# Two weight-remainder subtractions of the even mixer's output projection, moved from VectorE to GpSimd

## The chip, the cores and the metric

The kernel runs on one core of a Trainium2 chip. The metric is the device time of one execution in microseconds (us), the median of several runs. The core has five engines that work side by side and wait for one another through semaphores: TensorE (PE) for matmuls, VectorE (DVE), ScalarE (ACT), GpSimd (POOL) and SyncE (SP), which here only issues DMAs. SBUF is the working memory that all of them share; PSUM takes the matmul results, and its eight banks are called `ps` here.

## The reference

Two layers over 256 latent tokens and 256 context tokens of width 1024. Each layer is a half-step SwiGLU FFN, a mixer and a second half-step FFN. The even layer's mixer is the stage of this study:

```python
pl = hl @ w_in
a_l = silu(layernorm(depthwise_conv31(val * sigmoid(gate)) + b))   # 512 channels
q, k = rope(...); att_l = softmax(q k^T, window, context, sink) v  # 8 heads of 64
yl = concatenate([a_l, att_l]) @ w_out
```

The same is done for the context tokens. Everything is float32.

## The kernel before

**Products in three parts.** A float32 product is made of three faster ones. Both factors are split in a rounded high part (type fp32r) and the remainder: `hn_hi`, `hn_lo` for activations, `w_hi`, `w_lo` for weights. `three` (L491 to L493) issues hi by hi, lo by hi, hi by lo.

**Units of weights.** Weights come in units of up to 128 x 2048 elements. SP loads unit u into `raw[:, u % 2]` (L399), and waits for `lo_made >= u - 1` first, since the slot must be free. ACT copies it to `w_hi[:, u % 2]` (`head`, L989, semaphore `hi_made`), and DVE subtracts, `w_lo = raw - w_hi` (`rest`, `rest_of`, L1304, semaphore `lo_made`). PE waits for `lo_made` before it uses a unit. `E` is the first of the seven units of the even mixer's input projection, `E + 7` to `E + 10` are the four units of its output projection (`U["ev_out"]` is `E + 7`). They are used only after the attention and the LayerNorm of the convolution.

**The convolution.** 512 channels are four tiles of 128. Each of the 31 taps of tiles 0, 1 and 2 is one DVE instruction on 128 x 512 (`taps`, L1509 for a tile's first tap, L1512 for the others): `y = upad * weight + y`. The taps are issued in a fixed order, some ahead of the attention loop and some two or three at a time within it. Tile 3 is done by PE (`conv_turn`, L743): for each tap a matmul of a 128 x 128 diagonal of weights. GpSimd makes the 31 diagonals (`tensor_scalar` on the identity, L480) into 12 places. Diagonal n from 12 on waits until PE has used diagonal n - 12 (`turned_tap`).

**Before the attention.** DVE works through a list written out by hand: batches of taps, the rotary embedding, `w_lo` of units E + 4, E + 5, E + 6, then 12 taps, `gated_value(2)` (L1498, the gated input of tile 2), `w_lo` of E + 7, 12 taps, `gated_value(3)`, `w_lo` of E + 8, the negated sinks (L1553), and then the attention loop.

**The attention loop.** 16 steps j, one for a head pair, a stream and a query tile. In step j PE computes the scores of j + 1 (L706), two taps of tile 3 (L743) from j = 1 on, the transposes of step j - 1's weights (L720) and, in some steps, the products with the values (L734). DVE takes the row maxima (`largest`: L1563 or L1568, then L1570, which releases ACT), the denominators (L1577, L1578) and some taps. ACT computes the exponentials (L1130), normalises (L1143) and copies the transposes (L1152).

Of the kernel before, what the change touches and what calls it, by code (L numbers as in the profile page):

```python
# [44 lines left out]
ALU = mybir.AluOpType  # L45
# [17 lines left out]
def schedule():  # L63

    base, size = {}, []

    def add(name, n, elements):
        base[name] = len(size)
        size.extend([elements] * n)

    def ffn(name):
        for part, n in zip("AB", PARTS):
            add(f"{name}up{part}", n, UNIT)
            add(f"{name}down{part}", KT, n * P)

    ffn("f0")
    add("ev_in", 7, UNIT)
    add("ev_out", 4, UNIT)
    ffn("f1")
    ffn("f2")  # L80
    add("od_gate", 1, KT * 4 * HM)
    add("od_in", 16, UNIT)
    add("od_out", 4, UNIT)
    ffn("f3")
    return base, size


def build(nc, t, out):

    U, SIZE = schedule()  # L90
    NU = len(SIZE)
    with ExitStack() as ctx:
        def sb(name, shape, dt=F32, scope=ctx):
            return scope.enter_context(nc.sbuf_tensor(name, shape, dt))

        def sem(name):
            return ctx.enter_context(nc.semaphore(name))
# [5 lines left out]
        raw = sb("raw", [P, 2, UNIT])  # L103
        w_hi = sb("w_hi", [P, 2, UNIT], F32R)
        w_lo = sb("w_lo", [P, 2, UNIT], F32R)
# [55 lines left out]
        hi_made = sem("hi_made")  # L161
        lo_made = sem("lo_made")
# [122 lines left out]
        def bank(u, j=0):  # L285
            return 2 * (u % 2) + j
# [4 lines left out]
        def col(name, i, n=1):  # L291
            return cols[:, COLS[name][0] + i:COLS[name][0] + i + n]
# [35 lines left out]
        DIAGS = 12  # L328

        def diag_place(n):  # L330
            q = n % DIAGS
            return (acc, sd, rstd)[q // 4][:, q % 4 * P:(q % 4 + 1) * P]
# [126 lines left out]
        @block.gpsimd  # L459
        def _(pool):  # L460
            def vector_rows(i):

                q = i % SLOTS_MOD
                pool.dma_start(mod_raw[:, q, :], t["mod_w"][i]).then_inc(mod_in[q], 16)  # L464

            for i in range(SLOTS_MOD):
                pool.wait_ge(mod_mm, 5 + i // 2)
                vector_rows(i)
            pool.wait_ge(mod_mm, KT)
            pool.dma_start(c_row.rearrange("p s k -> p (s k)"), t["c_rows"].partition_broadcast(P))\  # L470
                .then_inc(c_rows_in, 16)
            for i in range(SLOTS_MOD, MOD_F0 + SLOTS_MOD):
                pool.wait_ge(mod_made, KT + i - SLOTS_MOD + 1)
                vector_rows(i)
            pool.wait_ge(mats_in, 16)
            pool.wait_ge(rstd_mm, 2)
            for n in range(CONV_W):
                if n >= DIAGS:
                    pool.wait_ge(turned_tap, n - DIAGS + 1)
                pool.tensor_scalar(diag_place(n), ident, col("conv_w", n * CT + 3), None, ALU.mult).then_inc(diag_ready, 1)  # L480
            for i in range(MOD_F0 + SLOTS_MOD, NMOD):
                pool.wait_ge(mod_made, KT + i - SLOTS_MOD + 1)
                vector_rows(i)
# [808 lines left out]
        def _(dve):  # L1292
# [8 lines left out]
            def rest(u0, r, n):  # L1301

                dve.wait_ge(hi_made, u0 + 2 * r + 1)
                dve.tensor_tensor(w_lo[:, u0 % 2, 0:n], raw[:, u0 % 2, 0:n], w_hi[:, u0 % 2, 0:n],  # L1304
                                  ALU.subtract).then_inc(lo_made, 1)

            def rest_of(u):
                if u < NU:
                    rest(u, 0, SIZE[u])
# [178 lines left out]
            E = U["ev_in"]  # L1488
# [5 lines left out]
            def gated_value(c, gate, b):  # L1494

                u = E + c if c < 2 else E + 3 + c
                dve.wait_ge(gate_made, CONV_G + c + 1)
                dve.tensor_tensor(upad[:, c, :, PAD:PAD + LAT], two_streams(gate), two_streams(ps[:, b, :]),  # L1498
                                  ALU.mult).then_inc(unit_evac, 1)

            def taps(a, b):

                for n in range(a, b):
                    c, i = TAP_ORDER[n]
                    if i == 0 and c in (0, 2):
                        dve.wait_ge(unit_evac, E + 2 if c == 0 else E + 6)
                    dst, src = two_streams(y[:, c, :]), upad[:, c, :, i:i + LAT]
                    if i == 0:
                        ins = dve.tensor_scalar(dst, src, col("conv_w", c), col("conv_b", c), ALU.mult, ALU.add)  # L1509
                    else:  # L1510
                        dve.wait_ge(tap_done, TAP_AT[c, i - 1] + 1)
                        ins = dve.scalar_tensor_tensor(out=dst, in0=src, scalar=col("conv_w", i * CT + c), in1=dst,  # L1512
                                                       op0=ALU.mult, op1=ALU.add)
                    ins.then_inc(tap_done, 1)
# [30 lines left out]
            rest_of(E + 6)  # L1545
            taps(EARLY, EARLY + 12)
            gated_value(2, t_ring[:, 0, :], bank(E + 5))
            rest_of(E + 7)
            taps(EARLY + 12, AHEAD_OF_LOOP)
            gated_value(3, t_ring[:, 1, :], bank(E + 6))  # L1550
            rest_of(E + 8)

            link(dve.tensor_scalar(att_cols[:, 4, 0:NH_ATT], col("sink", 0, NH_ATT), -1.0, None, ALU.mult))  # L1553

# [76 lines left out]
            u = U["od_gate"]  # L1631
# [4 lines left out]
            for d, s, tiles_of in ((0, 0, rows[:, 0, :, 2:4]), (0, 2, rows[:, 0, :, 0:2]), (1, 0, rows[:, 1, :, ::-1])):  # L1636
                n = tiles_of.shape[2]
# [106 lines left out]
            for n in range(16):  # L1744
                u = U["od_in"] + n
# [196 lines left out]
```

## Time and profile before

| | |
|---|---|
| median of 3 runs | 1844.24 us (1844.22 to 1845.74) |
| the profiled execution | 1850.17 us, of which the span is 1848.4 us |
| busy share of the span | PE 97%, DVE 62%, ACT 33%, POOL 5% |
| TensorE's granted clock, mean | 0.982 |
| the stage of the change, from the first gated value to the last attention product | 432 to 581 us of the span |

The span runs from the first to the last instruction of the profiled execution. Busy shares are means over stages with different limits, so a small edit has to be read from the stage in which it lies. Starts are in us from the beginning of the span. An instruction that follows another on its engine overlaps it a little in the records, so one of a row is read off the starts as well as the durations.

### The profile page before, as it was taken

Reading aid. Unit: us, or ns where it says so; the run is one execution under the profiler, and the core shown is the slowest. Engines: PE = TensorE matmul, PEld = TensorE weight load, DVE = VectorE, ACT = ScalarE, POOL = GpSimd, SP = SyncE. Lnnn points to the kernel's source line nnn. Section 1 sums busy time; section 2 is a strip of 40 time slices with the busy share of each in tenths; the row PEclk is TensorE's granted clock in tenths of the full one; section 3 lists DMA queues with packets and bytes.
Section 4 is the critical chain, followed back from the end, with each engine's and each line's share of the span. In section 5 each row is a group of like instructions: output and inputs, shape, how many; then the busy total and the mean of one; then the engine's idle time right before and its main releaser. Section 6 shows DMA issues by size and latency. Waiting matters only on the chain.

```text
span 1848.4 us, 23459 instructions
## 1 busy us (share of the span) xinstructions
PE 1787.1 (97%) x9265; PEld 1489.0 (81%) x9265; DVE 1142.1 (62%) x1735; ACT 617.0 (33%) x821; POOL 96.9 (5%) x164
## 2 busy tenths in 40 slices
PE   9999999999899999999999999999999999899996
PEld 5888888878545778888888788888888999899996
DVE  5578667875964557766787577433346436765554
ACT  4332223232375333212322322122223333454342
POOL 0011001020030001000110010000000000000000
PEclk8999999999899999999999999999999999999998
DMA  9455455542200225555555254332222222245552
GB/s 386 157 193 181 170 183 185 187 168 78 82 1 1 74 90 196 174 183 175 193 171 178 88 187 141 108 109 96 72 90 85 76 69 92 91 147 178 178 177 95
DMA packets 49040, 253.36 MB, mean 137 GB/s; under 512 B 5568, under 2 KB 7104, under 8 KB 32576
## 3 DMA queue, kind: packets, MB, share of 16 engines
q1 hardware_dynamic: 30384, 184.10, 28.8%
q0 software_dynamic: 18576, 68.17, 11.5%
q8 instruction: 54, 0.88, 0.2%
q14 instruction: 26, 0.21, 0.0%
HBM read 251.20 MB, written 1.05 MB: 136 GB/s over the span
## 4 chain that ended last, share of the span: by engine, by line
PE 88%; DVE 6%; ACT 4%; issue 1%; DMA 1%; SPq 0%; ACTq 0%; DVEq 0%
PE ps L491 27%; PE ps L493 27%; PE ps L492 27%; DVE w_lo L1304 2%; ACT w_hi L989 1%; DVE y L1512 1%; PE ps L857 1%; PE ps L886 1%; PE ps L743 1%; PE ps L720 1%; PE ps L521 1%; PE ps L734 1%; DVE t_ring L1360 0%; PE ps L706 0%; PE ps L546 0%
## 5 line engine op out<-in xcount | busy, mean ns | idle before, releaser
L491 PE MATMUL ps<-hn_hi,w_hi 128*128 128x512 f32 (+2 forms) x1784 | 645.0, 362 | 14.5 <-DVE hn_lo L1367 7.2
L492 PE MATMUL ps<-hn_lo,w_hi 128*128 128x512 f32 (+2 forms) x1784 | 638.7, 358 | 0.0
L493 PE MATMUL ps<-hn_hi,w_lo 128*128 128x512 f32 (+2 forms) x1784 | 638.5, 358 | 0.0
L1304 DVE TENSOR_TENSOR w_lo<-raw,w_hi 128x2048 fp32r<-128x2048 f32 (+2 forms) x184 | 376.9, 2048 | 349.2 <-ACT w_hi L989 349.0
L989 ACT ACTIVATE w_hi<-raw 128x2048 fp32r<-128x2048 f32 (+2 forms) x184 | 316.5, 1720 | 732.8 <-PE ps L493 726.5
L491 PEld LDWEIGHTS ps<-hn_hi,w_hi 128*128 128x128 f32 (+1 forms) x1784 | 337.9, 189 | 72.7 <-DVE hn_lo L1367 10.0
L493 PEld LDWEIGHTS ps<-hn_hi,w_lo 128*128 128x128 f32 (+1 forms) x1784 | 337.8, 189 | 50.1
L492 PEld LDWEIGHTS ps<-hn_lo,w_hi 128*128 128x128 f32 (+1 forms) x1784 | 337.8, 189 | 48.2 <-issue 0.5
L491 PE MATMUL ps<-a_hi,w_hi 128*128 128x512 f32 (+1 forms) x704 | 255.6, 363 | 2.6 <-DVE a_lo L1434 1.7
L492 PE MATMUL ps<-a_lo,w_hi 128*128 128x512 f32 (+1 forms) x704 | 255.3, 363 | 0.0
L493 PE MATMUL ps<-a_hi,w_lo 128*128 128x512 f32 (+1 forms) x704 | 255.2, 363 | 0.0
L1408 DVE CUSTOM_DVE_ANT_0 t_ring<-mod_raw,cols 128x1024 f32<-128x1024 f32 x128 | 163.9, 1280 | 1.8
L1408 DVE CUSTOM_DVE_ANT_0 mod_raw<-mod_raw,cols 128x1024 f32<-128x1024 f32 x128 | 163.9, 1281 | 0.0
L491 PEld LDWEIGHTS ps<-a_hi,w_hi 128*128 128x128 f32 x704 | 132.9, 189 | 23.6 <-DVE a_lo L1434 2.1
L493 PEld LDWEIGHTS ps<-a_hi,w_lo 128*128 128x128 f32 x704 | 132.9, 189 | 20.7
L492 PEld LDWEIGHTS ps<-a_lo,w_hi 128*128 128x128 f32 x704 | 132.9, 189 | 20.6
L1323 DVE SCALAR_TENSOR_TENSOR xT<-ps,modT,xT 128x256 f32<-128x256 f32 x136 | 59.9, 479 | 133.0 <-PE ps L493 132.9
L1048 ACT ACTIVATE a_hi<-prod 128x512 f32 (+3 forms) x88 | 50.9, 579 | 212.8 <-DVE prod L1431 212.8
L464 POOL DMA_DIRECT2D mod_raw<-in_mod_w x128 | 67.8, 530 | 900.8 <-DVE modT L1408 859.5
L1434 DVE TENSOR_TENSOR a_lo<-prod,a_hi 128x512 fp32r<-128x512 f32 (+1 forms) x88 | 55.0, 625 | 63.6 <-ACT a_hi L1048 63.6
L491 PE MATMUL ps<-w_hi,hn_hi 128*128 128x256 f32 x256 | 76.0, 297 | 0.0
L493 PE MATMUL ps<-w_hi,hn_lo 128*128 128x256 f32 x256 | 72.4, 283 | 0.0
(214 smaller groups left out, 1305.2 us busy)
## 6 DMA issues: line engine op xcount, KB each, us to landing
raw<-in_w_up SPq DMA_DIRECT2D x88, 1024.0 KB, 4.9
mod_raw<-in_mod_w POOLq DMA_DIRECT2D x128, 512.0 KB, 3.8
raw<-in_w_downA SPq DMA_DIRECT2D x32, 768.0 KB, 4.2
raw<-in_w_downB SPq DMA_DIRECT2D x32, 640.0 KB, 3.9
raw<-in_w_od_in SPq DMA_DIRECT2D x16, 1024.0 KB, 4.9
mod_raw<-in_mod_first SPq DMA_DIRECT2D x8, 1024.0 KB, 9.5
raw<-in_w_ev_in SPq DMA_DIRECT2D x7, 1024.0 KB, 5.1
raw<-in_w_ev_out SPq DMA_DIRECT2D x4, 1024.0 KB, 5.0
```

The source lines that it names most:

```text
L464: pool.dma_start(mod_raw[:, q, :], t["mod_w"][i]).then_inc(mod_in[q], 16)
L491: pe.matmul(o, lh, rh, start=first, stop=False)
L492: pe.matmul(o, lh, rl, start=False, stop=False)
L493: return pe.matmul(o, ll, rh, start=False, stop=last)
L521: last = pe.matmul(ps[32 * g:32 * g + 32, BLOCK_BANKS[b % 2], 0:LAT], c_act[:, 2 * g + i, :], block_place(b)[:, 2 * g + i, :], start=(i == ...
L720: last = pe.transpose(ps[:, 6 + h2, i * P:(i + 1) * P], weight_place(s)[:, h2, i * P:(i + 1) * P], ident)
L989: act.activation(w_hi[:, u0 % 2, 0:n], raw[:, u0 % 2, 0:n], ACT.Copy).then_inc(hi_made, 1)
L1048: act.activation(a_hi[:, j + 2 * r, 0:w], prod[:, j, 0:w], ACT.Copy).then_inc(a_hi_made, 1)
L1304: dve.tensor_tensor(w_lo[:, u0 % 2, 0:n], raw[:, u0 % 2, 0:n], w_hi[:, u0 % 2, 0:n], ALU.subtract).then_inc(lo_made, 1)
L1323: last = dve.scalar_tensor_tensor(out=xT[:, d0 + 2 * r, tokens(s)], in0=ps[:, bank(u0, b), tokens(s)], scalar=modT[:, vec, d0 + 2 * r, s:s ...
L1408: last = dve.tensor_tensor_reduce(out=spent, in0=mod_raw[:, q, :], in1=c_row[:, s, :], scale=1.0, scalar=col("mod_b", m * KT + k), op0=ALU ...
L1434: dve.tensor_tensor(a_lo[:, j + 2 * r, 0:w], prod[:, j, 0:w], a_hi[:, j + 2 * r, 0:w], ALU.subtract).then_inc(a_made, 1)
```

## The change

The subtractions for units E + 7 and E + 8 leave DVE's list. GpSimd makes them, one ahead of diagonal 12 and one ahead of diagonal 13. Each waits for the `lo_made` of the unit before and for ACT's `w_hi` of its own unit.

```diff
@@ gpsimd
             for n in range(CONV_W):
+                if n in (DIAGS, DIAGS + 1):
+                    u = U["ev_out"] + n - DIAGS
+                    pool.wait_ge(lo_made, u)
+                    pool.wait_ge(hi_made, u + 1)
+                    pool.tensor_tensor(w_lo[:, u % 2, :], raw[:, u % 2, :], w_hi[:, u % 2, :],
+                                       ALU.subtract).then_inc(lo_made, 1)
                 if n >= DIAGS:
                     pool.wait_ge(turned_tap, n - DIAGS + 1)
@@ vector
             taps(EARLY, EARLY + 12)
             gated_value(2, t_ring[:, 0, :], bank(E + 5))
-            rest_of(E + 7)
             taps(EARLY + 12, AHEAD_OF_LOOP)
             gated_value(3, t_ring[:, 1, :], bank(E + 6))
-            rest_of(E + 8)
```

## Rows read from the trace of the kernel before

**Rows 1.** The page: the chain that ended last, by engine

```profile
PE 88%; DVE 6%; ACT 4%; issue 1%; DMA 1%; SPq 0%; ACTq 0%; DVEq 0%
```

**Rows 2.** The chain in order of time, 487 to 507 us (start, us, what)

```profile
487.40 2.20 DVE w_lo L1304
...
497.94 2.20 DVE w_lo L1304
...
503.90 3.71 PE ps L743 x4
```

**Rows 3.** Busy us and count by engine in stretches, then granted clock, DMA share, GB/s

```profile
488.00:490.00 2.00, 2.00 (x10) 1.65 (x10) 2.00 (x3) 0.00 (x0) 0.00 (x0) 1.00 0.00 0
...
498.00:500.00 2.00, 0.00 (x0) 0.00 (x0) 2.00 (x1) 0.00 (x0) 0.00 (x0) 0.50 0.00 0
...
506.00:508.00 2.00, 2.00 (x5) 0.83 (x5) 1.93 (x9) 0.53 (x1) 0.90 (x2) 0.50 0.00 0
508.00:510.00 2.00, 1.94 (x11) 1.15 (x9) 1.16 (x2) 1.10 (x3) 0.85 (x1) 0.96 0.00 0
```

**Rows 4.** Timeline of ACT ahead of the loop (start, us, instruction)

```profile
480.01 1.91 ACT L989 ACTIVATE w_hi<-raw 128x2048 fp32r<-128x2048 f32 x1
491.64 0.60 ACT L1119 ACTIVATE t_ring<-ps 128x512 f32<-128x512 f32 x1 [9.72 <-PE ps L493]
...
494.05 1.28 ACT L1130 ACT_TABLE_LOAD   x1
```

**Rows 5.** Timeline of DVE ahead of the loop

```profile
478.77 8.03 DVE L1512 SCALAR_TENSOR_TENSOR y<-upad,cols,y 128x512 f32<-128x512 f32 x12
486.72 0.68 DVE L1498 TENSOR_TENSOR upad<-t_ring,ps 128x512 f32<-128x512 f32 x1
```

**Rows 6.** Timelines of POOL and DVE where a diagonal meets DVE's work

```profile
403.64 2.12 POOL L480 TENSOR_SCALAR acc<-mats,cols 128x128 f32<-128x128 f32 x1 [13.35 <-PE ps L558]
```

```profile
403.00 2.29 DVE L1304 TENSOR_TENSOR w_lo<-raw,w_hi 128x2048 fp32r<-128x2048 f32 x1 [0.83 <-ACT w_hi L989]
```

**Rows 7.** The same where DVE's instruction is the longer one, with its undisturbed like

```profile
536.22 0.60 POOL L480 TENSOR_SCALAR acc<-mats,cols 128x128 f32<-128x128 f32 x1 [0.26 <-PE ps L743]
```

```profile
536.27 0.86 DVE L1512 SCALAR_TENSOR_TENSOR y<-upad,cols,y 128x512 f32<-128x512 f32 x1
```

```profile
537.06 0.74 DVE L1512 SCALAR_TENSOR_TENSOR y<-upad,cols,y 128x512 f32<-128x512 f32 x1
```

```profile
517.38 0.78 DVE L1512 SCALAR_TENSOR_TENSOR y<-upad,cols,y 128x512 f32<-128x512 f32 x1
```

```profile
407.47 0.66 DVE L1367 SCALAR_TENSOR_TENSOR hn_lo<-t_ring,modT,hn_hi 128x256 fp32r<-128x256 f32 x1
```

```profile
409.35 0.48 DVE L1367 SCALAR_TENSOR_TENSOR hn_lo<-t_ring,modT,hn_hi 128x256 fp32r<-128x256 f32 x1
```

**Rows 8.** Timeline of all engines in the loop's first steps

```profile
506.00 0.60 POOL L480 TENSOR_SCALAR acc<-mats,cols 128x128 f32<-128x128 f32 x1 [92.38 <-PE ps L743]
...
507.39 0.16 DVE L1570 SCALAR_TENSOR_TENSOR att_cols<-att_cols 128x2 f32<-128x2 f32 x1
...
507.71 1.15 POOL L480 TENSOR_SCALAR acc<-mats,cols 128x128 f32<-128x128 f32 x1 [1.10 <-PE ps L743]
...
508.90 0.72 ACT L1130 ACTIVATE prod<-gact,att_cols 128x512 f32<-128x512 f32 x1 [2.37 <-PE ps L720]
```

**Rows 9.** Timeline of PE: taps at full clock, taps 12 and 13, first output unit

```profile
529.71 1.99 PE L743 MATMUL ps<-upad,rstd 128*128 128x512 f32 x4
...
534.14 1.13 PE L743 MATMUL ps<-upad,acc 128*128 128x512 f32 x2
```

```profile
584.10 0.80 PE L491 MATMUL ps<-hn_hi,w_hi 128*128 128x512 f32 x1
```

**Rows 10.** Timelines of SP and ACT: loads of E + 9, E + 10, first copy

```profile
489.63 10.87 SPq L399 DMA_DIRECT2D raw<-in_w_ev_out  x2
```

```profile
606.86 1.92 ACT L989 ACTIVATE w_hi<-raw 128x2048 fp32r<-128x2048 f32 x1 [2.61 <-PE ps L493]
```

## The prediction

> **What bounds the kernel now.** I read first the page's chain of work that ended last. It is 88% PE and 6% DVE [rows 1], so an edit on DVE is worth time only where DVE has its few per cent of the chain. The chain in order of time shows that this place is one of them. From 487 to 500 us it lies on DVE without a break, and both subtractions that the change removes are pieces of it, 2.20 us each [rows 2]. The table of stretches says the same from the other side: at 488 to 490 us PE is still full, at 498 to 500 us PE, ACT and POOL do nothing at all, DVE is full, and TensorE's granted clock has gone to 0.50 [rows 3]. So the start of the attention loop hangs on the DVE list alone.
>
> **Removed.** Two instructions by 2.20 us is 4.40 us. Is all of it there to be had? The next limits ahead of the loop are ACT's: the sigmoid for `gated_value(3)` starts at 491.64 us and lasts 0.60, and the load of the table for the exponential ends at 494.05 + 1.28 = 495.33 us [rows 4]. The loop can start when the second subtraction ends, at 497.94 + 2.20 = 500.14 us [rows 2]; 4.40 us earlier is 495.74, still behind both. So removal alone would give all 4.40 us, and the loop behind it is a chain of dependent steps that would start and end so much earlier.
>
> **Added, the first subtraction.** GpSimd has been idle since its twelfth diagonal. It starts when ACT's `w_hi` of E + 7 is there, at 480.01 + 1.91 = 481.92 us [rows 4]. DVE is then in a batch of 12 taps, 478.77 to 486.80 us [rows 5], each with two inputs in SBUF. Do the two engines disturb each other? The rows show two things. A diagonal that normally takes 0.60 us took 2.12 us when it started inside DVE's 2.29 us subtraction, and ended at 405.76, some 0.5 us after it [rows 6]. So GpSimd waits for a DVE instruction with two SBUF inputs. The other way round, the tap that begins as GpSimd reads takes 0.86 us against 0.74, another one 0.78 us, and an `hn_lo` piece 0.66 us against 0.48 [rows 7]. So a diagonal's read of 128 elements costs DVE 0.04, 0.12 or 0.18 us. The new instruction reads two inputs of 2048, 32 times as many elements: 1.3, 3.8 or 5.8 us. I take the middle, 3.8 us, and keep the other two for the range; below them stands no cost, if GpSimd fits its reads into the pauses between DVE's instructions. For the upper end there is also the whole 0.60 us of a diagonal by 16 for the length alone, 9.6 us. A block of B us here delays the taps and everything behind them by B, as DVE has no idle time up to the loop. With 3.8 us the start of the loop is at -4.4 + 3.8 = -0.6 us.
>
> The rows don't say whether DVE loses only the cycles of the reads or the whole of GpSimd's instruction. The Trainium skill, "SBUF — State Buffer", says that the pair of ports the two engines share is an exclusive lock for a whole instruction, also between a GpSimd instruction that reads SBUF and a DVE one with two SBUF inputs, and that whoever starts first keeps it. The skill's "GPSIMD Engine Reference" (section 3.1) gives 4497 ns for a two-input instruction of 2048 float32 elements, and advises VectorE for such work. No row of this trace has that instruction; by the page the block would be about 4.2 us as an estimate and the whole sum 0.8 us worse than mine.
>
> **Added, the second subtraction.** It stands behind diagonal 12, and that waits for PE's first tap, which is inside the loop. Diagonal 12 started at 506.00 us, with 0.26 us between two diagonals the next instruction would start at 506.86 us [rows 7, 8]. I let its reads begin 0.3 us later. DVE's instructions on PSUM and one SBUF input go on, but L1570 at 507.39 us [rows 8] has two SBUF inputs and waits: until 506.86 + 0.3 + 3.8 = 510.96, which is 3.57 us. Queued behind it on DVE are the denominators of step 1 and two taps; and ACT waits for L1570 with the exponentials of step 2, and PE with its transposes for ACT. These exponentials started at 508.90 us, held by PE's transposes and not by DVE [rows 8]; L1570 ended at 507.55, so 1.35 us of slack cover it. What is left is 3.57 - 1.35 = 2.2 us on the chain PE to ACT to PE, which has no later pause to make it up. In general the second block costs B - 1.6 us, and nothing below 1.6.
>
> **The diagonals behind.** Diagonal 13 came at 507.71 us and would come at about 511.5. PE uses the diagonals 12 and 13 at 534.14 us [rows 9], so some 20 us cover the delay; without this cover each us late would be a us of the loop. If GpSimd had to fetch code for another kind of instruction, that would be covered too.
>
> **The weights.** `w_lo` of E + 7 is first needed when PE begins the output projection at 584.10 us [rows 9], 70 us after the later of the two subtractions. SP's load of E + 9 waits for the first subtraction and that of E + 10 for the second: issues at 489.63 and 500.17 us now [rows 10], the latter would be at about 511. ACT copies E + 9 at 606.86 us [rows 10]. Nothing is queued behind these loads that is wanted earlier. Cost zero, covered by 90 us.
>
> **TensorE's clock.** It stood at 0.50 (1.2 GHz) in the stretches from 498 to 508 us, and was 0.96 in 508 to 510 [rows 3]. At that level the four matmul records of the first two taps cost 3.71 us on the chain [rows 2], and the same four at full clock 1.99 us [rows 9]. A stall in step 2 may keep the clock low for the next two taps too: up to 1.7 us. An earlier loop start might win a part of the low stretch. I put nothing in the sum and both in the range.
>
> **The sum.** -4.4 (removed) + 3.8 (first block) + 2.2 (second block past its slack) = +1.6 us. In general it is 2B - 6.0 us, zero at B = 3.0. The durations are from the profiled execution, 1850.17 us with a span of 1848.4 and 1.8 us around it; it lies 5.9 us above the median of the runs, which I take as a constant of the profiler. On the median: 1844.24 + 1.6 = 1845.8 us.
>
> **Rivals.**
> - *GpSimd slips into DVE's pauses.* GpSimd is the one that waits, and DVE keeps its pace; the diagonals inside tap batches lengthened few taps and by little [rows 7], which speaks for it. Against it: a diagonal reads 128 elements and may just fit a pause, 4096 can't. With no delay 1844.24 - 4.4 = 1839.8 us; with 0.12 us on each of the 12 taps 1841.3; with B = 1.3 us, 1841.1. It ends beyond 0.2% only with less than 0.7 us of delay in all.
> - *The block is long.* One mechanism: DVE stands still while GpSimd reads, at 482 and at 507 us. From B = 4.9 us on the sum is over +3.7 us. At 5.8 us it is -4.4 + 5.8 + 4.2 = +5.6, 1849.8 us; at 9.6 us +13.2, 1857.4 us. For it speaks the `hn_lo` row [rows 7], against it the two tap rows.
> - *The clock stays low in step 2.* On top of my forecast: 1845.8 + 1.7 = 1847.5 us.
> - *The change does nothing*, since the attention's start hangs on something else. Only PE, idle, and ACT, done at 495.33, are there [rows 3, 4]. 1844.2 us, hardly possible.
>
> **How the numbers follow.** A change of 0.2%, 3.7 us, is about what a measurement of this kernel can tell from none. Forecast (B between 1.6 and 4.9 us, with or without the clock's part): 0.5. GpSimd in the pauses: 0.25, of which 0.17 with nearly no delay. The long block: 0.22. No effect: 0.03. So faster 0.18, same 0.56, slower 0.26 (0.04 of it from the clock on top of the forecast). The range reaches down to the gain without any block, 1839.8, and up to the block of 5.8 us, 1849.8. The likeliest case alone spans 1841.5 to 1848.
>
> **What would show it.** In the profile after: the two GpSimd instructions at about 482 and 506 to 507 us; a gap or one long tap of about 3.8 us in DVE's batch of 12 (right), or 12 taps in 8.0 us as now (the first rival); the loop's first L1563 at about 499.6 us (495.8 for the first rival); L1570 of step 2 held to about 510.5, and the exponentials behind it waiting for DVE and not for PE. I am wrong if GpSimd's instruction takes much more than 5 us, if DVE runs through it, or if GpSimd gets its turn only when the tap batch is over.

## The result, and the profile after

The changed kernel takes 1848.57 us (median of 20 runs, 1843.9 to 1853.87) against 1844.37 us (20 runs, 1841.83 to 1849.25): a ratio of 1.0020, with a 95% interval of 1.0013 to 1.0027. That is 3.7 us slower (2.4 to 5.0) by the ratio, 4.2 us by the medians. The forecast was +1.6 us. The time lies in its range, but 1.2 us from the upper end of it (1849.8), and 0.6 us above the 1848 up to which I had put the likeliest case alone. The loss is also at the 3.7 us from which I had reckoned the long block.

Everything that the prediction spoke of stands in the timelines between 475 and 510 us. Lines 476 on are moved by the edit: L486 of after is L480 of before, L1310 is L1304, L1504 is L1498, L1515 and L1518 are L1509 and L1512, L1567 is L1563, L1574 is L1570, L1136 is L1130, L749 is L743; L482 is the new subtraction. Kernels with other edits are moved by a few lines more. First GpSimd (start, us, instruction, what ended the idle time before it):

```profile
480.48 9.22 POOL L482 TENSOR_TENSOR w_lo<-raw,w_hi 128x2048 fp32r<-128x2048 f32 x1 [68.43 <-ACT w_hi L995]
503.55 0.78 POOL L486 TENSOR_SCALAR acc<-mats,cols 128x128 f32<-128x128 f32 x1 [13.85 <-PE ps L749]
504.30 4.51 POOL L482 TENSOR_TENSOR w_lo<-raw,w_hi 128x2048 fp32r<-128x2048 f32 x1
508.79 2.59 POOL L486 TENSOR_SCALAR acc<-mats,cols 128x128 f32<-128x128 f32 x3
```

Then VectorE over the same stretch:

```profile
475.00 2.28 DVE L1310 TENSOR_TENSOR w_lo<-raw,w_hi 128x2048 fp32r<-128x2048 f32 x1
477.20 8.04 DVE L1518 SCALAR_TENSOR_TENSOR y<-upad,cols,y 128x512 f32<-128x512 f32 x12
485.14 0.69 DVE L1504 TENSOR_TENSOR upad<-t_ring,ps 128x512 f32<-128x512 f32 x1
485.87 4.12 DVE L1515 TENSOR_SCALAR y<-upad,cols 128x512 f32<-128x512 f32 x1
...
497.99 0.69 DVE L1567 CUSTOM_DVE_ANT_0 gact<-ps,att_mask 128x512 f32<-128x512 f32 x1
...
505.12 3.72 DVE L1574 SCALAR_TENSOR_TENSOR att_cols<-att_cols 128x2 f32<-128x2 f32 x1
```

And ScalarE's exponentials of step 2, which in [rows 8] waited for PE:

```profile
508.87 0.72 ACT L1136 ACTIVATE prod<-gact,att_cols 128x512 f32<-128x512 f32 x1 [4.61 <-DVE att_cols L1574]
```

The reader is to see three things. GpSimd alone needs 4.51 us for what VectorE does in 2.28; its first subtraction took 9.22 us, because it got nothing while the 12 taps ran, which kept their 8.04 us [rows 5]. It was served behind them, beside `gated_value(2)` (489.70 - 4.51 = 485.19 us, an estimate), and then VectorE's tensor_scalar lasted 4.12 us instead of 0.54. That tensor_scalar reads one 128 x 512 tensor and a column of weights, so an instruction needn't read two large tensors from SBUF to be held; `gated_value(2)`, with one input in SBUF and one in PSUM, took its usual 0.69 us. The second one stopped an instruction on two columns, L1574, for 3.72 us instead of 0.16, up to the end of GpSimd's instruction (504.30 + 4.51 = 508.81; 505.12 + 3.72 = 508.84).

The table of stretches of after has a piece that was not in before (stretch and its length in us; busy us and count of PE, its weight loads, VectorE, ScalarE, GpSimd; then TensorE's granted clock, DMA share, GB/s): PE idles while it waits for step 2, and the clock falls to 0.50 once more.

```profile
508.00:510.00 2.00, 0.70 (x2) 0.00 (x0) 1.97 (x5) 1.14 (x3) 2.00 (x3) 1.00 0.39 53
510.00:512.00 2.00, 0.00 (x0) 0.00 (x0) 1.93 (x6) 2.00 (x7) 1.38 (x2) 1.00 0.70 274
512.00:514.00 2.00, 1.40 (x6) 0.76 (x8) 1.45 (x3) 1.13 (x4) 0.00 (x0) 0.84 0.48 201
514.00:516.00 2.00, 2.00 (x5) 0.50 (x2) 0.89 (x3) 2.00 (x7) 0.00 (x0) 0.50 0.00 0
```

### The profile page after: what moved, and what is told of

Read it like the earlier page. It is cut to its first block, busy times and chain, and to the rows that moved or that the text cites. A ratio compares the mean times of both kernels' runs of the same rounds, so it can differ in the third digit from the quotient of the medians.

```text
span 1849.8 us, 23461 instructions
## 1 busy us (share of the span) xinstructions
PE 1784.0 (96%) x9265; PEld 1487.6 (80%) x9265; DVE 1145.1 (62%) x1733; ACT 617.1 (33%) x821; POOL 109.9 (6%) x166
## 4 chain that ended last, share of the span: by engine, by line
PE 87%; DVE 6%; ACT 4%; DMA 1%; issue 1%; SPq 0%; ACTq 0%; DVEq 0%
PE ps L497 27%; PE ps L498 27%; PE ps L499 27%; DVE w_lo L1310 1%; ACT w_hi L995 1%; DVE y L1518 1%; PE ps L863 1%; PE ps L892 1%; DMA mod_raw<-in_mod_first 1%; PE ps L749 1%; PE ps L726 1%; PE ps L740 1%; PE ps L552 1%; PE ps L712 0%; DVE t_ring L1366 0%
## 5 line engine op out<-in xcount | busy, mean ns | idle before, releaser
L1310 DVE TENSOR_TENSOR w_lo<-raw,w_hi 128x2048 fp32r<-128x2048 f32 (+3 forms) x182 | 372.4, 2046 | 347.7 <-ACT w_hi L995 347.5
```

## A ruler for the stage

Single profiles reach this stage up to 4.6 us apart, so I measure within it. The ruler has four parts, taken as differences of starts in each kernel's timelines: **a** from `w_lo` of E + 6 to the loop's first L1563; **b** from there to the exponentials of step 2; **c** from there to those of step 4; **d** from there to the LayerNorm's first VectorE instruction. **Stage** ends at the first residual of the output projection (L1323, 606.87 us in before) and contains 22.2 us more. For before, a is 500.26 - 476.57 = 23.69. Ratios are to the runs of the kernel before on the same chip.

| kernel | a | b | c | d | stage | ratio (95% interval) |
|---|---|---|---|---|---|---|
| before | 23.69 | 8.64 | 8.86 | 66.94 | 130.30 | |
| before_again | 23.70 | 7.52 | 8.86 | 66.93 | 129.25 | 0.9996 (0.9986 to 1.0005) |
| after | 22.99 | 10.88 | 9.96 | 66.94 | 132.97 | 1.0020 (1.0013 to 1.0027) |
| after_again | 23.77 | 10.88 | 9.96 | 66.94 | 133.75 | 1.0020 (1.0009 to 1.0031) |
| no_sub | 19.50 | 7.65 | 8.86 | 66.93 | 125.15 | 0.9980 (0.9971 to 0.9989) |
| first_only | 25.97 | 8.13 | 8.87 | 66.93 | 132.13 | 1.0021 (1.0011 to 1.0031) |
| second_only | 21.50 | 10.88 | 9.90 | 66.93 | 131.41 | 1.0021 (1.0013 to 1.0030) |
| dve_in_loop | 19.41 | 8.10 | 8.85 | 66.93 | 125.52 | 0.9979 (0.9970 to 0.9987) |
| half | 21.56 | 8.72 | 8.86 | 66.94 | 128.28 | 0.9995 (0.9987 to 1.0004) |
| pieces | 19.91 | 7.52 | 8.85 | 66.95 | 125.46 | 0.9977 (0.9967 to 0.9987) |
| after_busy | 23.77 | 10.89 | 8.87 | 66.93 | 132.67 | 1.0006 (0.9997 to 1.0014) |
| write_only | 19.42 | 7.71 | 8.86 | 66.94 | 125.13 | one run |
| one_input | 22.80 | 10.00 | 11.35 | 66.94 | 133.31 | one run |

Part d is the same in all: behind step 4 nothing of the change is left. What the change does lies in a, b and c. Outside of the stage the profiles differ too, without a pattern by edit: 471.9 to 476.6 us ahead of it and 1237 to 1244 us behind it.

## The experiments

**What there was to win (no_sub).** Edit of before:

```diff
+            def mark_of(u):
+                dve.wait_ge(hi_made, u + 1)
+                dve.tensor_tensor(w_lo[:, u % 2, 0:8], raw[:, u % 2, 0:8], w_hi[:, u % 2, 0:8],
+                                  ALU.subtract).then_inc(lo_made, 1)
...
-            rest_of(E + 7)
+            mark_of(E + 7)
...
-            rest_of(E + 8)
+            mark_of(E + 8)
```

> The two subtractions shrink to 8 of 2048 columns and stay on VectorE in their old places; the rest of the work of these two units is left out, GpSimd gets nothing. This shows how much there was to win. Theory 1 (the loop's start hangs on VectorE's list, both 2.20 us pieces are on the chain): 4.1 us faster than before, about 1840.3, the first L1563 4.1 us earlier after w_lo of E+6. Rival (something else holds the loop's start, so nothing was ever to be had, and the change only added waits): 0 to 1 us faster.

1840.3 us, 3.7 us faster (2.0 to 5.3). Part a fell by 4.19 us, as the two shortened pieces ask. So the loop's start does hang on VectorE's list and all of it comes through to the end; "the change does nothing" falls, and so does a gain that something else holds back.

**The first subtraction alone (first_only).** Edit of after:

```diff
-                if n in (DIAGS, DIAGS + 1):
+                if n == DIAGS:
...
             gated_value(3, t_ring[:, 1, :], bank(E + 6))
+            dve.wait_ge(lo_made, E + 8)
+            rest_of(E + 8)
```

> Only the subtraction ahead of diagonal 12 is GpSimd's, the one of E+8 stays on VectorE in its old place. Theory 1 (VectorE's tensor_scalar stands still for 3.6 us, 2.2 us won): 1.4 us slower than before, about 1845.8. Rival (the first block costs nothing, all of the loss is in the loop): 2.2 us faster.

Here GpSimd was served in the middle of the 12 taps. Timeline of VectorE, then of GpSimd:

```profile
475.93 12.38 DVE L1518 SCALAR_TENSOR_TENSOR y<-upad,cols,y 128x512 f32<-128x512 f32 x12
```

```profile
479.22 5.23 POOL L482 TENSOR_TENSOR w_lo<-raw,w_hi 128x2048 fp32r<-128x2048 f32 x1 [66.87 <-ACT w_hi L995]
```

The batch of taps lasts 12.38 us instead of 8.04: a hold of 4.3 us, against 2.2 us saved. Part a is 2.28 us longer, where 1.4 was expected from the first profile's 3.6. The hold is 4.3 us in both; in after 0.7 us of it lay beside `gated_value(2)` (485.14 to 485.83 us), which has one SBUF input and was not stopped. The rival, a first block for nothing, falls. By the ratio the kernel is 3.9 us slower (2.0 to 5.7); its stage is 1.8 and 2.9 us longer than in the two profiles of before.

**The second alone (second_only).** Edit of after:

```diff
-                if n in (DIAGS, DIAGS + 1):
+                if n == DIAGS + 1:
...
+            rest_of(E + 7)
             taps(EARLY + 12, AHEAD_OF_LOOP)
```

> Only the subtraction ahead of diagonal 13 is GpSimd's, the one of E+7 stays on VectorE in its old place. Theory 1 (L1570 of step 2 waits 3.6 us, 2.2 us of it past the slack, 2.2 us won ahead of the loop, and TensorE's clock falls once more after the stall for about 1 us): 0 to 1.3 us slower than before, 1844.4 to 1845.7. Rival (the whole loss of the change comes from the clock that falls in the stall): 2.5 us slower or more.

Part a is 2.20 us shorter, exactly one subtraction, b is 10.88 as in after, and c 9.90. The stage is 1.1 to 2.2 us longer than in the two profiles of before. By the ratio it is 3.9 us slower (2.4 to 5.5), above what was expected and above the 2.5 us that I had set for the rival. The stage decides against that rival all the same: c, where the clock falls, grew by 1.04 us, and b by 2.2 to 3.4. In first_only the runs lie 1 to 2 us above what the stage accounts for, in second_only 1.7 to 2.8. By the ratios the two halves add up to 7.8 us, against 3.7 for both together; by the stages they add up to 2.9 to 5.0 against 2.7 to 4.5. So the excess lies outside of the stage, and where it comes from stays open.

**VectorE after all, in another place (dve_in_loop).** Edit of before; the two `rest_of` ahead of the loop go:

```diff
                 taps(taps_by(j - 1) if j else AHEAD_OF_LOOP, taps_by(j))
+                if j in (6, 10):
+                    rest_of(E + (7 if j == 6 else 8))
```

> VectorE makes both subtractions after all, but within the attention loop, behind the taps of steps 6 and 10, where it stood idle 2.8 and 3.4 us before; nothing is left out. Theory 1 (the place counts, and only the chain ahead of the loop and the port made the change slow): 4.4 us faster than before, about 1840.0, 8 us faster than the changed kernel. Rival (a subtraction of 2.2 us in the loop delays a maximum and so the chain): same as before or up to 2 us slower.

1840.99 us, 3.9 us faster than before (2.4 to 5.5), and within 0.4 us as short in the stage as no_sub, which left the work out. The timeline of VectorE shows the cover: behind the first of the two, the maximum of the next step still waits for PE's scores. Behind the second (536.23 us) it waits 1.18 us.

```profile
517.48 2.28 DVE L1304 TENSOR_TENSOR w_lo<-raw,w_hi 128x2048 fp32r<-128x2048 f32 x1
520.36 0.69 DVE L1566 TENSOR_REDUCE att_cols<-ps 128x2 f32<-128x512 f32 x1 [0.59 <-PE ps L706]
```

So the idea behind such a move, to take these 4.4 us off the chain ahead of the loop, is sound; it is the place and the engine that failed.

**Half the length (half).** Edit of after:

```diff
-                    pool.tensor_tensor(w_lo[:, u % 2, :], raw[:, u % 2, :], w_hi[:, u % 2, :],
+                    h = UNIT // 2
+                    pool.tensor_tensor(w_lo[:, u % 2, 0:h], raw[:, u % 2, 0:h], w_hi[:, u % 2, 0:h],
```

> The changed kernel with GpSimd's two subtractions on 1024 of the 2048 columns each; the other halves are left out. Theory 1 (VectorE stands still for as long as GpSimd reads, so the block goes with the length: 4.3 us for a whole one, 2.15 us for half): the loop's start 4.4 - 2.15 = 2.2 us earlier than before (up to 2.9), L1570 of step 2 held 1.5 us, 0.2 us past its slack: 2 us faster than before, about 1842, 6 us faster than the changed kernel. Rival (a fixed cost of each handover between the engines, or the wait behind a diagonal, makes the loss): as slow as the changed kernel, less than 1.5 us gained on it.

Timeline of GpSimd and of VectorE:

```profile
503.28 2.35 POOL L483 TENSOR_TENSOR w_lo<-raw,w_hi 128x1024 fp32r<-128x1024 f32 x1
```

```profile
477.61 10.17 DVE L1519 SCALAR_TENSOR_TENSOR y<-upad,cols,y 128x512 f32<-128x512 f32 x12
...
504.10 1.56 DVE L1575 SCALAR_TENSOR_TENSOR att_cols<-att_cols 128x2 f32<-128x2 f32 x1
```

And of PE, the first taps and the transposes for which step 2's exponentials wait as well:

```profile
500.54 3.78 PE L750 MATMUL ps<-upad,acc 128*128 128x512 f32 x4
504.11 1.43 PE L727 MATMUL ps<-mats,prod 128*128 128x128 f32 x8
```

The taps lose 2.13 us instead of 4.34, L1575 (L1570 of before) takes 1.40 us more than its 0.16 instead of 3.56 more, up to the end of GpSimd's instruction in both, and a is 2.1 us shorter than in before: the hold goes with the length, and no fixed cost shows in it. The 1.40 us are covered to 0.1: the taps ran at the low clock, as in the first profile of before, and PE's transposes ended at 505.54 us, L1575 at 505.66. The gain over before is 0.9 us (-0.7 to 2.4), less than the 2 us expected; the stage is 1.0 to 2.0 shorter. The rival fell, since it is 4.3 us faster than after_again, on the same chip, by the medians.

**Sixteen pieces (pieces).** Edit of after:

```diff
-                if n in (DIAGS, DIAGS + 1):
-                    u = U["ev_out"] + n - DIAGS
-                    pool.wait_ge(lo_made, u)
-                    pool.wait_ge(hi_made, u + 1)
...
+                if n in range(DIAGS, DIAGS + 16):
+                    u, piece = U["ev_out"] + (n - DIAGS) // 8, (n - DIAGS) % 8
+                    if piece == 0:
+                        pool.wait_ge(lo_made, u)
+                        pool.wait_ge(hi_made, u + 1)
+                    part = slice(256 * piece, 256 * (piece + 1))
+                    cut = pool.tensor_tensor(w_lo[:, u % 2, part], raw[:, u % 2, part], w_hi[:, u % 2, part],
+                                             ALU.subtract)
+                    if piece == 7:
+                        cut.then_inc(lo_made, 1)
```

> The changed kernel with each of GpSimd's subtractions cut in 8 pieces of 256 columns, one ahead of each of the diagonals 12 to 27; nothing is left out. All pieces now fall in the loop. Theory 1 (the lock lasts one instruction, and the chain has about 1.3 us of slack at VectorE's maxima in every second step): a piece holds VectorE 0.55 us at most and is mostly covered, 4.4 us won ahead of the loop and 0 to 2 us lost in it: 1840 to 1842. Rival (every piece shows on the chain, 16 by 0.55 us): 1848, as slow as the changed kernel.

1840.99 us, 4.2 us faster than before (2.4 to 6.1). One piece, not none as I wrote, still falls ahead of the loop and makes the 12 taps 8.52 us long; the others hold VectorE's instructions by up to some 0.5 us each. Its timeline around one of them:

```profile
507.65 0.46 DVE L1578 SCALAR_TENSOR_TENSOR att_cols<-att_cols 128x2 f32<-128x2 f32 x1
508.29 2.53 DVE L1522 SCALAR_TENSOR_TENSOR y<-upad,cols,y 128x512 f32<-128x512 f32 x3
```

L1578 (L1570 of before) takes 0.46 us instead of 0.16, and three taps 2.53 instead of 2.06 to 2.09, and b, c and d show none of it. The same GpSimd work, 2 by 2048 columns, costs 0.5 us ahead of the loop (a is 19.91, against 19.41 in dve_in_loop) and nothing in it, as long as no single hold is longer than the slack it meets.

**The kernel before, once more (before_again).** No edit.

> The kernel before, unchanged, once more: its profile and times against its own. The first profile of it lies 5.8 us above the median of its runs, that of the changed kernel only 3.0 us. Theory 1: a profiled run is one of the spread of runs, and this one shows a shorter even mixer stage or a shorter start, by as much as TensorE's clock is less often at 0.50 in them; ratio 1.000. Rival: the profiler adds a constant of about 6 us, and stage and start are as in the first profile.

1844.27 us against 1844.55, the ratio 1.000 within its interval, and this profiled execution has a span of 1842.5 us, 5.9 us less than the first. Part b is 7.52 us, not 8.64. The timelines of PE and VectorE, and of ACT, say why:

```profile
500.26 2.86 PE L743 MATMUL ps<-upad,acc 128*128 128x512 f32 x4
```

```profile
503.82 0.16 DVE L1570 SCALAR_TENSOR_TENSOR att_cols<-att_cols 128x2 f32<-128x2 f32 x1
```

```profile
504.21 0.72 ACT L1130 ACTIVATE prod<-gact,att_cols 128x512 f32<-128x512 f32 x1 [1.24 <-PE ps L720]
```

TensorE's clock was back earlier, the four records of the first taps took 2.86 us instead of 3.78 (3.71 on the chain [rows 2]), and L1570 ended 0.2 us before the exponentials that wait for it, not 1.35 us. So the 1.35 us of slack that I had read in [rows 8] belong to a profile with a slow clock; here there are 0.2. And the profiler adds no constant of 5.9 us: a profiled run is one of the spread.

**The changed kernel, once more (after_again).** No edit.

> The changed kernel once more, same chip as the other three. Theory 1: GpSimd's first subtraction gets the port either in the batch of 12 taps (which then lasts 12.3 us instead of 8.0) or behind it (4.1 us instead of 0.5 for the tensor_scalar), 4.3 or 3.6 us in all, the second one holds L1570 for 3.6 us in either case; 3 to 5 us slower than before. Rival: the first subtraction is always served last, as in the first profile.

1849.38 us, again a ratio of 1.0020. GpSimd was served inside the taps this time (5.23 us, taps 12.38 us), so a is 23.77; b and c are those of after.

**The clock's part (after_busy).** Edit of after, in PE's loop behind `conv_turn`:

```diff
+                if j == 2:
+                    pe.wait_ge(lo_made, E + 8)
+                    for _ in range(14):
+                        pe.matmul(ps[:, 1, :], w_hi[:, (E + 7) % 2, 0:P], w_hi[:, (E + 7) % 2, 0:TOK],
+                                  start=True, stop=True)
```

> The changed kernel with 14 matmuls more on TensorE in step 2 of the loop, behind its two taps, into a bank that nobody reads: they fill 3.2 of the 3.9 us for which PE waits there. Nothing is left out. Theory 1 (VectorE's stalls cost 7.2 to 7.9 us against 4.4 saved and 1.3 of slack, and on top TensorE's clock falls after the stall and makes the next taps 0.9 us longer): the clock stays at 1.00 in step 3, the four tap records there take 2.0 us instead of 2.85, about 1 us faster than the changed kernel, still 2.5 to 4 us slower than before. Rival (the clock is the main part of the loss): as fast as before.

The timeline of PE, with the taps of step 3 in the last line (2.85 us in after):

```profile
508.61 3.78 PE L767 MATMUL ps<-w_hi 128*128 128x512 f32 x14
513.10 0.63 PE L726 MATMUL ps<-mats,sq 128*128 128x128 f32 x4 [0.71 <-ACT pT_full L1163]
513.65 1.13 PE L712 MATMUL ps<-qk 64*128 64x512 f32 x4
514.71 1.99 PE L749 MATMUL ps<-upad,sd 128*128 128x512 f32 x4
```

Part c is 8.87 us, as without the change, and a and b are those of after_again: the second fall of the clock costs 1.09 us here, and it is PE's stall that brings it. The kernel takes 1846.38 us, 1.1 us above before by the ratio (-0.6 to 2.6) and 1.75 by the medians; that is more regained than the 1 us that I expected, and the rest of it lies outside the stage.

**What GpSimd reads (write_only, one_input).** In place of the subtraction a memset of the same 128 x 2048, and `w_lo = 0.5 * raw`:

```diff
-                    pool.tensor_tensor(w_lo[:, u % 2, :], raw[:, u % 2, :], w_hi[:, u % 2, :],
-                                       ALU.subtract).then_inc(lo_made, 1)
+                    pool.memset(w_lo[:, u % 2, :].bitcast(F32), 0.0).then_inc(lo_made, 1)          # write_only
+                    pool.tensor_scalar(w_lo[:, u % 2, :], raw[:, u % 2, :], 0.5, None, ALU.mult).then_inc(lo_made, 1)  # one_input
```

> GpSimd's two subtractions are replaced by a memset of w_lo to 0, which reads nothing; the remainders of these two units are left out. Theory 1 (VectorE's instructions with two SBUF inputs need the shared read path, so only a GpSimd instruction that reads SBUF stops them): taps in 8.0 us and L1574 of step 2 in 0.16 us although the memset runs beside them, even mixer stage 4 to 5 us shorter than before. Rival (any GpSimd instruction on SBUF stops VectorE for its length): both are stretched by its 2 us or so.

> GpSimd's two subtractions are replaced by w_lo = 0.5 * raw, one input of 2048 instead of two; the right remainders of these two units are left out. Theory 1 (VectorE stands for as long as GpSimd's reads last): GpSimd's instruction takes 2.0 to 2.7 us instead of 4.5, the 12 taps last about 10, L1574 of step 2 is held 1.2 to 1.7 us instead of 3.6. Rival (the hold does not depend on what is read): 3.6 us and more as in the changed kernel.

write_only, GpSimd and VectorE:

```profile
480.21 1.81 POOL L482 MEMSET w_lo<- 128x2048 f32 x1 [66.81 <-ACT w_hi L994]
500.45 1.80 POOL L482 MEMSET w_lo<- 128x2048 f32 x1
```

```profile
476.95 8.03 DVE L1517 SCALAR_TENSOR_TENSOR y<-upad,cols,y 128x512 f32<-128x512 f32 x12
...
501.29 0.16 DVE L1573 SCALAR_TENSOR_TENSOR att_cols<-att_cols 128x2 f32<-128x2 f32 x1
```

one_input, the same:

```profile
502.38 5.36 POOL L482 TENSOR_SCALAR w_lo<-raw 128x2048 fp32r<-128x2048 f32 x1
```

```profile
475.46 11.41 DVE L1518 SCALAR_TENSOR_TENSOR y<-upad,cols,y 128x512 f32<-128x512 f32 x12
...
503.19 2.83 DVE L1574 SCALAR_TENSOR_TENSOR att_cols<-att_cols 128x2 f32<-128x2 f32 x1
```

The memset ran wholly beside VectorE's two-input instructions and held none, and the stage is 4.1 and 5.2 us shorter than in the two profiles of before: it is GpSimd's reading that stops them. My figure for one input was wrong: the instruction takes 5.36 us, more than the two-input one (4.51), the taps lose 3.4 us, and L1574 is released at 506.02 us, 3.6 us after GpSimd's start and 1.7 before its end. So the hold isn't simply the number of elements read. One thing more stands in this profile: PE waits only 2.61 us for step 2, but c is 11.35 us, 2.5 us more than in before, and the taps of step 3 take 3.62 us. Timeline of PE, then the table of stretches:

```profile
509.80 1.09 PE L726 MATMUL ps<-mats,sq 128*128 128x128 f32 x4 [2.61 <-ACT pT_full L1158]
510.81 2.08 PE L712 MATMUL ps<-qk 64*128 64x512 f32 x4
512.82 3.62 PE L749 MATMUL ps<-upad,sd 128*128 128x512 f32 x4
```

```profile
508.00:510.00 2.00, 0.20 (x1) 0.24 (x2) 1.93 (x7) 1.65 (x3) 2.00 (x3) 0.83 0.59 139
510.00:512.00 2.00, 2.00 (x8) 0.99 (x7) 0.69 (x1) 1.02 (x5) 0.38 (x1) 0.50 0.91 385
...
514.00:516.00 2.00, 2.00 (x4) 0.74 (x3) 1.93 (x7) 0.07 (x1) 0.84 (x1) 0.50 0.00 0
```

So a shorter wait can bring a longer low stretch, and what the clock costs is not fixed at 1.1 us.

## Why the prediction was right or wrong

**The chain.** Right. VectorE's list sets the loop's start, and the removal, predicted at 4.40 us, is worth 4.28 in part a of dve_in_loop (4.19 in no_sub, which keeps 8 columns).

**The first block.** The mechanism was right, the size close: 3.8 us predicted from 32 times a delay of 0.12, measured 4.3 us, of which 3.6 or 4.3 show, by whether GpSimd is served behind the taps or among them. The size was partly luck: the same scaling by elements read gives 16 times 0.12, 1.9 us, for one_input, and 3.4 us were measured. And two of my signs of being wrong came true in the first profile, a GpSimd instruction of much more than 5 us (9.22) and a turn only when the tap batch was over. The sum stood it because VectorE's next instruction was then held for nearly as long. In six of the seven profiles in which GpSimd's first instruction reads SBUF it was served among the taps. Part a came out at -0.7 and +0.1 us for -0.6 predicted. The Trainium skill, "SBUF — State Buffer" (Who interferes with whom), has an exclusive lock for a whole instruction. The hold up to the end of GpSimd's subtraction agrees; one_input's hold, which ends 1.7 us before the instruction does, doesn't, so the trace agrees in part. That whoever starts first keeps the ports fits the subtractions' holds. It doesn't say that a waiting instruction comes next: in after, the taps ran on for over 4 us ahead of a waiting GpSimd. The Trainium skill, "GPSIMD Engine Reference" (section 3.1), gives 4497 ns for the instruction; the trace agrees with 4.51 us.

**The second block.** The hold was right, 3.57 us predicted and 3.56 measured (3.72 - 0.16), though two misses cancel in it: the hold ends 4.5 us after GpSimd's start and not 4.1, and L1574 comes 0.82 us after that start and not 0.53. **The step that failed is the slack taken from it**, 1.35 us. It came from one profile in which the first taps ran at 1.2 GHz for 3.78 us; in before_again it is 0.2 us. The term is then 10.88 - 7.52 = 3.4 us instead of 2.2. In the seven profiles without a long hold in step 2, part b runs from 7.52 to 8.64 us, and the one that I had read is the longest; so the term is 2.2 to 3.4 us, by the clock that the first taps meet, and the forecast took its lowest value.

**The clock.** It was left out of the sum and priced at up to 1.7 us on the range. It falls in all three profiles with a hold of 3.6 us in step 2 and no filler, and costs 1.0 to 1.1 us; after_busy shows that for one of them. In one_input it costs 2.5 us after a shorter wait. It belonged in the sum, as the stall was forecast. The 1848 us that I gave as the top of the likeliest case leaves it out as well, though the chance of that case takes it in.

**The sum again.** Against before_again: -4.3 (removed) + 4.3 (the hold among the taps) + 3.4 (second hold) + 1.1 (clock) = +4.5 us, which is the stage's 133.75 - 129.25; with GpSimd served behind the taps, +3.7 us. The ratio says 3.7 us. Against the first profile of before alone the change would seem to cost only 2.7 us.

**The rivals.** GpSimd in VectorE's pauses is refuted as a way out: even where it let the taps pass, it took the port behind them. The long block is refuted in its size, 4.3 us and not 5.8. The clock that stays low came true in a somewhat later place, at the taps of step 3. The covers held: the diagonals 13 to 15 were ready at 511.4 us, over 20 us before their use, and neither SP's loads nor the output projection waited, as part d and the rest of the stage show.

**The reading of the profile's own time.** I took its 5.9 us over the median as a constant of the profiler. It is not: before_again's span is 1842.5 us at a median of 1844.3.

## What to carry to other kernels

A helper engine whose reads hold up the busy one doesn't take work off it when the work comes in one long instruction: it hands back the time as holds, here 4.3 us for 2.2 saved, and these fall on whatever is next, even on two columns that ScalarE waits for. Look first for idle time of the same engine behind the critical stretch (3.9 us faster here), or cut the helper's work in pieces shorter than the slack that they meet (4.2 us faster). And read a slack from more than one profile, above all beside a stretch in which TensorE's clock is low.

## What the runs showed of the hardware that I had not expected

A GpSimd tensor_scalar of 128 x 2048 from one input (5.36 us) is slower than its subtraction of two (4.51 us), though one of 128 x 128 takes 0.60, and a memset of that size 1.80. It lets VectorE go 1.7 us before it ends. A waiting GpSimd instruction is sometimes served between two taps (5.23 us in all) and sometimes not in 4 us of them (9.22 us), from one run of the same kernel to the next. And in after, a stall of 3.9 us of PE brought its clock down to 0.50 only when PE already worked again: 1.00 at 510 to 512 us, 0.50 at 514 to 516. In one_input a wait of 2.61 us was enough, the clock was 0.83 already at 508 to 510 us, in the wait, and 0.50 up to 516.
